# A quarter of each low part in the stage over v moves from VectorE to GpSimd

## The chip, the cores and the metric

The kernel runs on one core of a Trainium2 chip. A core has five engines that work side by side and wait for each other through semaphores: TensorE (PE; its weight loads are listed apart as PEld), VectorE (DVE), ScalarE (ACT), GpSimd (POOL) and SyncE (SP), which here only issues transfers. The metric is the device time of one execution in microseconds (us); lower is better. It is measured as the median of several executions. A profile is one execution, and its own time stands beside its span (first to last instruction).

## The reference

Two transformer blocks over a sequence of 512 tokens with 1024 features. The first block has a stick-breaking attention, a short convolution and a mixture of experts. The second block has attention, a Hyena filter and, at its end, the PEER layer, in which the change lies:

```python
def chunk(xc):                                   # 128 tokens
    q = (xc @ wq).reshape(PEER_CHUNK, PEER_HEADS, 2, half)
    s1 = jnp.einsum('chd,hnd->chn', q[:, :, 0], keys1)
    s2 = jnp.einsum('chd,hnd->chn', q[:, :, 1], keys2)
    ...                                          # 16 best pairs for each token and head: eidx, g
    a = jnp.einsum('chkd,cd->chk', u_tab[eidx], xc)
    wgt = (jax.nn.gelu(a) * g)
    return jnp.einsum('chk,chkd->cd', wgt, v_tab[eidx])
```

u_tab and v_tab have 16384 rows of 1024 numbers each.

## The kernel before, in words

For 384 of the 512 tokens the kernel does not gather rows. It multiplies by the whole of u and later by the whole of v, with a weight matrix that is zero where an expert was not chosen. For the other 128 tokens it gathers the rows of u and of v that each token needs, with indirect transfers that GpSimd issues (one transfer brings one row of 1024 for each of the 128 tokens, 0.5 MB; there are 128 for u and 128 for v).

**Parts.** A product in float32 is made of three products of a faster type, fp32r. Each operand is split in a high part (the value rounded to fp32r) and a low part (the value minus its high part). A *unit* is a tile of 128x2048 of wq, u or v. SP loads it in `RAW[n % 2]`; ScalarE makes the high part (`high`, line 1858) and VectorE the low part (`low`, one subtraction of 128x2048 through the helper `tt`, line 592), both in `PART[n % 2]`; TensorE then works on it. There are 8 units of wq, 64 of u and 64 of v. Everything is double buffered: `high(n)` and `low(n)` wait until TensorE has finished unit n-2, SP reloads `RAW` for unit n when the low part of unit n-2 is done.

**The stage over v** (from about 2146 us) has 32 steps of two units. For each unit TensorE makes 36 matmuls of 128x512 (lines 2648 to 2650). Here the first unit of a step is called the even unit and the second the odd one. The order of the work on every engine is one list written by hand, `V_STEPS`, that each engine's program walks through and of which it takes what is its own:

```python
for n in range(32):
    V_STEPS.append(("part", v_unit[n] + 1))          # odd unit of step n
    ...
    V_STEPS += [late.pop(0) for _ in range(2) if late] or [sums.pop(0) for _ in range(2) if sums]
    if n + 1 < 32:
        V_STEPS.append(("up", n + 1))
        V_STEPS.append(("part", v_unit[n] + 2))      # even unit of step n + 1
    V_STEPS += [late.pop(0) for _ in range(2) if late] or [sums.pop(0) for _ in range(4 if n % 3 == 0 else 3) if sums]
    V_STEPS.append(("down", n))
```

- "part": ScalarE `high`, VectorE `low`, SP the load of a later unit.
- "up": VectorE multiplies the tile `GIN` by the weights `WRB` (four instructions gin<-gin,wr of 128x384), ScalarE makes its high part `GE` (line 1944), VectorE its low part (four instructions ge<-gin,ge). SP loads `WRB` and `GIN` of a later step (`chunk`).
- "ud": a dot product of a gathered row of u (line 1375), in steps 0 to 5, four in each.
- "sv": a weighted sum of a gathered row of v (`row_sum`, line 600, tmp<-ug or vg,sparse,tmp, 128x1024). There are 128, in the steps after, five or six in each: two after the low part of the odd unit, and three (four in every third step) after the low part of the even unit. GpSimd, at the same place of its own list, issues the gather of the row eight sums later (`row_of_v`, line 2663), which waits until VectorE has made that sum.
- "down": the matmuls of the step.

In every instruction of VectorE named here both tensor inputs lie in SBUF.

**The other place that the diff touches** is far ahead, in the stage over the experts: ScalarE issues a load of ctx (1 MB, line 1639, semaphore `cx`) and four small loads of filter weights (lines 1640 to 1643, semaphore `lay`), and later squares ctx (`squares(10, ...)`, line 1488).

Of the kernel before, what the change touches and what calls it, by code (L numbers as in the profile page):

```python
# [74 lines left out]
def program(nc, A, out):  # L75
# [10 lines left out]
    ctx = ExitStack()  # L86
    with ctx:
# [5 lines left out]
        def sem(name):  # L93
# [2 lines left out]
        s = {n: sem("s_" + n) for n in (  # L96
            "const par z_v zd x0 x1 x2 x3 nsq nmm nv nw h_v pj_mm pj_a hn_v cv sc_a ada_v ada_mm ada_a att_mm att_a att_v "
            "mg_mm mg_v op_mm op_v wr rt_mm rt_v rt_a ht_mm ht_a hd mi_mm mi_a mi_v mu_mm mu_a mu_v mt_mm mm_v md_mm md_a md_v "
            "gx0 gx1 gx2 ys0 ys1 ys2 cx lay rope ly_mm ly_v ly_a xg xw xp xa xv xy gy0 gy1 gy2 gy3 cb_mm cb_v "
            "kv_mm kk_a hm_a kp_mm ro_mm ro_v w4_key fl_mm fl_v fl_a hp_mm hp_a hp_v tt_mm tt_a sp_mm sp_a sp_v iv_mm iv_v "  # L100
            "s2_mm e2_a a2_v tr_mm tr_a tr_v pv_mm pv_a gt_mm gt_a m2_mm m2_v o2_mm o2_v "
            "rw0 rw1 un_hi un_lo h2_v hr_a fx_mm fx_a gt0 gt1 gt2 gt3 sc_mm sc2_a tk_v tk_a tx_mm wg_v wg_mm wg_a ws0 ws1 "
            "wq0 wq1 gin0 gin1 gm_v ge_a vd_mm hs_a hs_mm ud_v ug0 ug1 ug2 ug3 sw_v vg0 vg1 vg2 vg3 ys_v y2_v fo_v out "
            "w0 w1 w2 w3 w4 w5 ph_a ph_v").split()}

# [416 lines left out]
        UNIT += [("v", c, h) for c in range(32) for h in range(2)]  # L522

        UNIT_DONE, n_fx, n_vd = [], 0, 0
        for kind, c, half in UNIT:
            if kind == "v":
                n_vd += 3
                UNIT_DONE.append(("vd_mm", n_vd))
            else:
                n_fx += 2  # L530
                UNIT_DONE.append(("fx_mm", n_fx))
# [56 lines left out]
        def vector_program(eng):  # L588
            dve = Port(eng)

            def tt(out_, in0, in1, op):
                return v.tensor_tensor(out=out_, in0=in0, in1=in1, op=op)  # L592
# [633 lines left out]
            def low(n):  # L1226
                if n < len(UNIT):
                    if n >= 2:
                        dve.wait_ge(s[UNIT_DONE[n - 2][0]], UNIT_DONE[n - 2][1])
                    dve.wait_ge(s["un_hi"], n + 1)  # L1230
                    hi, lo = PART[n % 2]
                    tt(lo, RAW[n % 2], hi.bitcast(f32), SUB).then_inc(s["un_lo"], 1)

            norm(18, 1.0 / D, S)
            for k in range(8):
# [221 lines left out]
            for half in range(2):  # L1457
                for q in (1, 3):
                    dve.wait_ge(s["vd_mm"], 6 * 31 + 3 * half + q)
                    dve.wait_ge(s["un_lo"], len(UNIT))  # L1460
                    if half and q == 3:
                        for d in (1, 2, 3):
                            sum_square(d, PA4, PV4)
                    v.tensor_copy(YT[q][:, 512 * half:512 * half + 512], bank[2 * (q - 1) + half]).then_inc(s["sw_v"], 1)
                for j in range(4):
                    d = 4 * half + j
                    dve.wait_ge(s["hs_mm"], 2 + d + 1)
                    stt(X[:, d, :], bank[(0, 2, 4, 6)[j] + half], MOD[:, 40 + d, 0:1], X[:, d, :], MUL, ADD).then_inc(s["y2_v"], 1)
                    if half and j:
                        sum_square(d - 1, PA4, PV4)  # L1470
                if half:
                    sum_square(7, PA4, PV4)
# [6 lines left out]
        def scalar_program(eng):  # L1479
# [156 lines left out]
            def layers(kind, li):  # L1636
                if kind == "dma" and li == 0:
                    act.wait_ge(s["op_mm"], 8)
                    a.dma_start(CX, A["ctx"].rearrange("p (k n) -> p k n", k=8)).then_inc(s["cx"], 16)
                    a.dma_start(ZF[0:33, :], A["zf"]).then_inc(s["lay"], 16)  # L1640
                    a.dma_start(FW1[0:33, :], A["hf_w1"]).then_inc(s["lay"], 16)
                    a.dma_start(FW2[0:64, :], A["hf_w2"]).then_inc(s["lay"], 16)
                    a.dma_start(FW3[0:64, :], A["hf_w3"]).then_inc(s["lay"], 16)
                if kind == "ctx":
                    squares(10, [CX[:, k, :] for k in range(8)], 256, lambda i: (s["cx"], 16))
                    root(10, 256)
                    act.wait_ge(s["ada_v"], 4)
                    for k in range(8):
                        act.wait_ge(s["h_v"], 17 + k)
                        a.activation(HC[:, k, :], HC[:, k, :], ACT.Identity, bias=MOD[:, k, 1:2]).then_inc(s["hm_a"], 1)  # L1650
                if kind == "sin":
                    act.wait_ge(s["ly_v"], 7 * li + 7)
                    a.activation(HM[0:64, :], ft[0][0:64, :], ACT.Sin).then_inc(s["ly_a"], 1)
                if kind == "dma" and li == 1:
                    act.wait_ge(s["ly_mm"], 3)
                    a.dma_start(COS, A["rope"][0]).then_inc(s["rope"], 16)
                    a.dma_start(SIN, A["rope"][1]).then_inc(s["rope"], 16)
                    a.dma_start(SKB, A["skip"]).then_inc(s["rope"], 16)
# [309 lines left out]
            for half in range(2):  # L1968
                act.wait_ge(s["vd_mm"], 6 * 31 + 3 * half + 2)
                act.wait_ge(s["un_lo"], len(UNIT))  # L1970
                if half:
                    square_chunks(19, "y2_v", PA4, PV4, 0, 4)
                a.activation(YT[2][:, 512 * half:512 * half + 512], bank[2 + half], ACT.Copy).then_inc(s["hs_a"], 1)
# [5 lines left out]
        def tensor_program(eng):  # L1979
# [223 lines left out]
            def layers(kind, li):  # L2203
                if kind == "ctx":
                    norm(10, ones, 256)
                if kind == "mm":
                    pe.wait_ge(s["lay"], 64)
                    pe.wait_ge(s["nv"], 41)
                    pe.wait_ge(s["ly_a"], li)
                    w, kk, src = ((FW1, 33, ZF), (FW2, 64, HM), (FW3, 64, HM))[li]  # L2210
                    t.matmul(bank[7][0:64, :], w[0:kk, :], src[0:kk, :], start=True, stop=True).then_inc(s["ly_mm"], 1)
# [419 lines left out]
            for kind, n in V_STEPS:  # L2631
# [3 lines left out]
                for half in range(2):  # L2635
                    unit = v_unit[n] + half
                    wh, wl = (k4(x) for x in PART[unit % 2])
                    pe.wait_ge(s["un_lo"], unit + 1)
                    pe.wait_ge(s["gm_v"], 8 * n + 8)
                    pe.wait_ge(s["fx_a"], len(fx_of))  # L2640
                    pe.wait_ge(s["sc2_a"], 16)
# [17 lines left out]
        def pool_program(eng):  # L2659
# [44 lines left out]
            def row_of_v(k):  # L2704
                if k < 128:
# [6 lines left out]
                        gp.wait_ge(s["wg_mm"], 96)  # L2712
                    rows(VG[(k + 4) % 8], A["v"], EID[:, k:k + 1], s[f"vg{k % 4}"])

            for kind, *i in ORDER3 + V_STEPS:
                if kind == "ud":
                    for k in range(4) if i[0] == 0 else (i[0] + 3,):
                        row_of_u(k)
                elif kind in ("vr", "sw"):
                    for k in range(4) if kind == "vr" else range(4, 8):  # L2720
                        row_of_v(k)
                elif kind == "sv":
                    row_of_v(i[0] + 8)


        def sync_program(eng):
# [66 lines left out]
            def unit(n):  # L2793
# [6 lines left out]
                    src = A["vd"][2 * c + half]  # L2800
                if n >= 2:
                    sp.wait_ge(s["un_lo"], n - 1)
                nc.sync.dma_start(RAW[n % 2], src).then_inc(s[f"rw{n % 2}"], 16)

            sp.wait_ge(s["o2_mm"], 8)
# [172 lines left out]
```

## Time and profile before

| what | value |
|---|---|
| median of 3 runs | 2714.17 us (2713.97 to 2717.03) |
| the profiled execution: time, span | 2714.08 us, 2712.3 us |
| mean granted clock of TensorE | 0.963 |
| busy over the span | PE 2480.9 us (91%), DVE 1712.5 us (63%), ACT 1044.2 us (38%), POOL 403.0 us (15%) |
| VectorE's low parts, all 136 units | 311.2 us, 2289 ns each |
| ScalarE's high parts, all 136 units | 260.5 us, 1915 ns each |

In the rows below a line of a timeline is: start (us from the span's start), duration (us), engine, line of the kernel, operation, output<-inputs, count; and in brackets the idle time of the engine just before and what ended it. Instructions of one engine that follow each other overlap a little in the records, so the step from start to start is the time that one costs in a chain. "part" is `PART`, "raw" is `RAW`, "P" is a PSUM bank, "tmp" is the sum over v, "ug" and "vg" are the eight buffers of gathered rows, "sparse" holds the weights of the sums.

### The profile page before, as it was taken

What the parts mean: (1) busy time and instruction counts of PE and PEld (TensorE: products, weight loads), DVE (VectorE), ACT (ScalarE), POOL (GpSimd) and SP (SyncE); (2) the same over time, 40 slices, a digit from 0 to 9 for tenths busy, and PEclk for the clock granted to TensorE, in tenths of its full rate; (3) what the DMA queues carried; (4) which work ended last, traced back from release to release, by engine and by line L of the source; (5) the groups of instructions that cost most, each with busy time, mean ns of one, the idle gap of its engine ahead of it and who ended that gap; (6) DMA issues with size and microseconds to landing.
All of it is one profiled execution on the core that took longest, in us unless ns stands there. A gap on an engine that the chain in (4) does not pass through costs nothing.

```text
span 2712.3 us, 31160 instructions
## 1 busy us (share of the span) xinstructions
PE 2480.9 (91%) x12293; PEld 1883.7 (69%) x12293; DVE 1712.5 (63%) x2974; ACT 1044.2 (38%) x1307; POOL 403.0 (15%) x299
## 2 busy tenths in 40 slices
PE   6998999587877989999989999989999999999996
PEld 4665676433333434577768999989999988777775
DVE  4524235412116556665642998889999478888886
ACT  4844532220104321377332433436555333333333
POOL 0100000000001000000000011232343134444430
PEclk9999999698986999999999999999999999999998
DMA  4443442499992100211122367769989799999992
GB/s 196 172 162 124 162 179 95 155 383 424 426 383 99 62 31 1 93 63 39 56 93 93 131 216 239 251 233 326 340 347 344 285 383 363 380 381 380 383 369 93
DMA packets 159215, 605.96 MB, mean 223 GB/s; under 512 B 13687, under 2 KB 79351, under 8 KB 126360
## 3 DMA queue, kind: packets, MB, share of 16 engines
q1 hardware_dynamic: 91104, 384.32, 37.8%
q0 software_dynamic: 42480, 154.68, 15.3%
q10 hardware_dynamic: 25480, 64.90, 6.1%
q8 instruction: 99, 1.62, 0.2%
q14 instruction: 52, 0.43, 0.0%
HBM read 533.08 MB, written 70.78 MB: 223 GB/s over the span
## 4 chain that ended last, share of the span: by engine, by line
PE 51%; DVE 21%; DMA 13%; issue 10%; ACT 4%; POOL 1%; ACTq 0%; SPq 0%; DVEq 0%; POOLq 0%
DVE window L592 6%; PE P L2544 4%; PE P L2545 4%; PE P L2546 4%; PE P L2200 4%; DVE part L592 3%; DMA ug<-in_v,sparse 3%; PE P L2375 3%; DVE ug L1375 3%; DMA H<-in_w_up 3%; PE P L2003 2%; DMA vg<-in_v,sparse 2%; PE P L2004 2%; PE P L2005 2%; DVE tmp L600 2%
## 5 line engine op out<-in xcount | busy, mean ns | idle before, releaser
L592 DVE TENSOR_TENSOR part<-raw,part 128x2048 fp32r<-128x2048 f32 x136 | 311.2, 2289 | 166.3 <-ACT part L1858 166.2
L2544 PE MATMUL P<-hr,part 128*128 128x384 f32 (+1 forms) x1136 | 397.8, 350 | 17.8 <-DVE part L592 17.1
L2546 PE MATMUL P<-hr,part 128*128 128x384 f32 (+1 forms) x1136 | 392.3, 345 | 0.0
L2545 PE MATMUL P<-hr,part 128*128 128x384 f32 (+1 forms) x1136 | 392.2, 345 | 0.0
L2663 POOL DMA_INDIRECT ug<-in_ur,sparse x128 | 177.5, 1387 | 1216.1 <-DVE window L1267 754.3
L2648 PE MATMUL P<-part,ge 128*128 128x512 f32 x768 | 301.8, 393 | 10.5 <-DVE part L592 9.8
L1858 ACT ACTIVATE part<-raw 128x2048 fp32r<-128x2048 f32 x136 | 260.5, 1915 | 101.7 <-PE P L2650 82.3
L2649 PE MATMUL P<-part,ge 128*128 128x512 f32 x768 | 299.1, 389 | 0.0
L2650 PE MATMUL P<-part,ge 128*128 128x512 f32 x768 | 298.9, 389 | 0.0
L2544 PEld LDWEIGHTS P<-hr,part 128*128 128x128 f32 x1136 | 215.3, 189 | 28.8 <-DVE part L592 22.9
L2545 PEld LDWEIGHTS P<-hr,part 128*128 128x128 f32 x1136 | 215.2, 189 | 4.8
L2546 PEld LDWEIGHTS P<-hr,part 128*128 128x128 f32 x1136 | 214.9, 189 | 4.9
L592 DVE TENSOR_TENSOR arena<-arena,P 128x512 f32<-128x512 f32 (+3 forms) x100 | 56.8, 577 | 207.6 <-ACT arena L1634 135.4
L2648 PEld LDWEIGHTS P<-part,ge 128*128 128x128 f32 x768 | 144.1, 188 | 49.0 <-DVE part L592 18.7
L1930 ACT ACTIVATE gt<-P 128x384 f32<-128x384 f32 x128 | 62.9, 492 | 296.8 <-PE P L2546 296.6
L1944 ACT ACTIVATE ge<-gin 128x384 fp32r<-128x384 f32 x128 | 65.5, 526 | 262.0 <-DVE gin L592 261.5
L2650 PEld LDWEIGHTS P<-part,ge 128*128 128x128 f32 x768 | 144.2, 188 | 30.2
L2649 PEld LDWEIGHTS P<-part,ge 128*128 128x128 f32 x768 | 144.2, 188 | 29.2
L1375 DVE SCALAR_TENSOR_TENSOR ug<-ug,ht 128x1024 f32<-128x1024 f32 x128 | 154.9, 1218 | 6.9 <-DMA ug<-in_ur,sparse 6.8
L2200 PE MATMUL P<-W,arena 128*64 128x512 f32 x384 | 124.8, 635 | 16.6 <-DMA H<-in_w_up 10.5
L592 DVE TENSOR_TENSOR window<-window 128x1024 bf16<-128x1024 bf16 (+6 forms) x198 | 118.4, 648 | 1.5
L2663 POOL DMA_INDIRECT vg<-in_v,sparse x64 | 101.6, 1588 | 116.0 <-DVE tmp L600 102.4
(359 smaller groups left out, 4483.7 us busy)
## 6 DMA issues: line engine op xcount, KB each, us to landing
raw<-in_u SPq DMA_DIRECT2D x64, 1024.0 KB, 5.3
raw<-in_vd SPq DMA_DIRECT2D x64, 1024.0 KB, 8.0
W<-in_w_up SPq DMA_DIRECT2D x24, 2048.0 KB, 18.3
W<-in_w_in SPq DMA_DIRECT2D x18, 2048.0 KB, 8.5
W<-in_ada_w SPq DMA_DIRECT2D x12, 2048.0 KB, 7.8
a_scratch<-gt ACTq DMA_DIRECT2D x128, 192.0 KB, 3.9
w_scratch<-window ACTq DMA_DIRECT2D x12, 2048.0 KB, 13.1
wr<-w_scratch SPq DMA_DIRECT2D x32, 768.0 KB, 13.4
```

The costliest lines, as they stand in the source:

```text
L592: return v.tensor_tensor(out=out_, in0=in0, in1=in1, op=op)
L1375: v.scalar_tensor_tensor(out=UG[k % 4], in0=UG[k % 4], scalar=1.0, in1=HT0, op0=MUL, op1=MUL, accum_out=DOT[:, k:k + 1]).then_inc(s["ud_v" ...
L1858: a.activation(PART[n % 2][0], RAW[n % 2], ACT.Copy).then_inc(s["un_hi"], 1)
L2200: ins = t.matmul(bank[2 + i % 2][xs, :], XT[i % 2][:, k, xs], w[:, k, :], start=k == 0, stop=k == 7)
L2375: ins = t.matmul(bank[n % 2], w[:, k, (n % 4) * 128:(n % 4) * 128 + 128], H[:, k, :], start=k == 0, stop=k == 7)
L2544: t.matmul(b, wh[:, k, js], HR[0][:, k, lo:S], start=k == 0, stop=False)
L2545: t.matmul(b, wh[:, k, js], HR[1][:, k, lo:S], start=False, stop=False)
L2546: ins = t.matmul(b, wl[:, k, js], HR[0][:, k, lo:S], start=False, stop=k == 7)
L2648: t.matmul(b, gh[:, k, qs], wh[:, k, :], start=n == 0 and k == 0, stop=False)
L2649: t.matmul(b, gh[:, k, qs], wl[:, k, :], start=False, stop=False)
L2650: ins = t.matmul(b, gl[:, k, qs], wh[:, k, :], start=False, stop=n == 31 and k == 3)
L2663: return g.indirect_dma_start(out=dst, out_offset=None, in_=src, in_offset=bass.IndirectOffsetOnAxis(ap=idx, axis=0)).then_inc(sem_, 16)
```

## The change

In the stage over v GpSimd makes columns 1536 to 2047 of the low part, and VectorE columns 0 to 1535. This holds for 63 of the 64 units; the first is left whole (`po_lo` gives 0 for it). GpSimd's instruction is queued at the place of "part" in its list and waits, as VectorE's does, for unit n-2 of TensorE and for the high part. It counts a semaphore of its own, `po_lo`, and all that waited for VectorE's half wait for it too: TensorE's matmuls of the unit, SP's reload of `RAW`, and at the end VectorE and ScalarE before they write over `RAW`. To have a semaphore for it, the load of ctx gives up its own (`cx`) and counts in `lay` with the four small loads, so that ScalarE's squares now wait for all five.

```diff
@@ -522,6 +522,7 @@
         UNIT_DONE, n_fx, n_vd = [], 0, 0
+        po_lo = lambda n: max(0, n - v_unit[0])
@@ -1229,7 +1230,8 @@
                     dve.wait_ge(s["un_hi"], n + 1)
                     hi, lo = PART[n % 2]
-                    tt(lo, RAW[n % 2], hi.bitcast(f32), SUB).then_inc(s["un_lo"], 1)
+                    m = 1536 if po_lo(n) else 2048
+                    tt(lo[:, 0:m], RAW[n % 2][:, 0:m], hi[:, 0:m].bitcast(f32), SUB).then_inc(s["un_lo"], 1)
@@ -1458,6 +1460,7 @@
                     dve.wait_ge(s["un_lo"], len(UNIT))
+                    dve.wait_ge(s["po_lo"], po_lo(len(UNIT) - 1))
@@ -1636,13 +1639,13 @@
-                    a.dma_start(CX, A["ctx"].rearrange("p (k n) -> p k n", k=8)).then_inc(s["cx"], 16)
+                    a.dma_start(CX, A["ctx"].rearrange("p (k n) -> p k n", k=8)).then_inc(s["lay"], 16)
...
-                    squares(10, [CX[:, k, :] for k in range(8)], 256, lambda i: (s["cx"], 16))
+                    squares(10, [CX[:, k, :] for k in range(8)], 256, lambda i: (s["lay"], 80))
@@ -1968,6 +1971,7 @@
                 act.wait_ge(s["un_lo"], len(UNIT))
+                act.wait_ge(s["po_lo"], po_lo(len(UNIT) - 1))
@@ -2204,7 +2208,7 @@
-                    pe.wait_ge(s["lay"], 64)
+                    pe.wait_ge(s["lay"], 80)
@@ -2636,6 +2640,8 @@
                     pe.wait_ge(s["un_lo"], unit + 1)
+                    if po_lo(unit):
+                        pe.wait_ge(s["po_lo"], po_lo(unit))
@@ -2712,7 +2718,16 @@
+            def low(n):
+                if n < len(UNIT):
+                    gp.wait_ge(s[UNIT_DONE[n - 2][0]], UNIT_DONE[n - 2][1])
+                    gp.wait_ge(s["un_hi"], n + 1)
+                    hi, lo = PART[n % 2]
+                    g.tensor_tensor(out=lo[:, 1536:2048], in0=RAW[n % 2][:, 1536:2048], in1=hi[:, 1536:2048].bitcast(f32), op=SUB).then_inc(s["po_lo"], 1)
+
             for kind, *i in ORDER3 + V_STEPS:
+                if kind == "part":
+                    low(*i)
@@ -2800,6 +2815,8 @@
                 if n >= 2:
                     sp.wait_ge(s["un_lo"], n - 1)
+                    if po_lo(n - 2):
+                        sp.wait_ge(s["po_lo"], po_lo(n - 2))
```

## Rows read from the trace of the kernel before

**Rows 1.** The windows of the stage: dots, sums, the last steps.

```profile
core 0: us, PE busy (x) PEld busy (x) DVE busy (x) ACT busy (x) POOL busy (x), PEclk, DMA share, GB/s
2126.00:2236.00 110.00, 108.72 (x503) 92.54 (x502) 79.13 (x107) 38.84 (x42) 34.76 (x24) 1.00 0.92 337
2241.40:2641.00 399.60, 390.35 (x1700) 317.02 (x1699) 353.84 (x360) 134.88 (x140) 187.56 (x124) 1.00 1.01 378
2641.00:2674.50 33.50, 33.50 (x148) 27.46 (x147) 24.40 (x27) 11.96 (x13) 0.00 (x0) 1.00 0.43 150
```

**Rows 2.** Who waited for whom in the sums' stretch: total us, times, longest us.

```profile
DVE part L592 <- ACT part L1858: 33.3, 25, 1.7
...
PEld P L2648 <- DVE part L592: 17.4, 22, 1.7
...
PE P L2648 <- DVE part L592: 9.2, 7, 1.3
```

**Rows 3.** VectorE's timeline: first, one whole, a longer and last of 23 steps with sums.

```profile
2257.84 2.29 DVE L592 TENSOR_TENSOR part<-raw,part 128x2048 fp32r<-128x2048 f32 x1 [1.32 <-ACT part L1858]
...
2343.36 2.29 DVE L592 TENSOR_TENSOR part<-raw,part 128x2048 fp32r<-128x2048 f32 x1 [1.32 <-ACT part L1858]
2345.57 4.06 DVE L600 SCALAR_TENSOR_TENSOR tmp<-ug,sparse,tmp 128x1024 f32<-128x1024 f32 x3
2349.55 2.29 DVE L592 TENSOR_TENSOR part<-raw,part 128x2048 fp32r<-128x2048 f32 x1
2351.75 2.67 DVE L600 SCALAR_TENSOR_TENSOR tmp<-vg,sparse,tmp 128x1024 f32<-128x1024 f32 x2
2354.34 1.02 DVE L592 TENSOR_TENSOR gin<-gin,wr 128x384 f32<-128x384 f32 x2
...
2359.91 2.29 DVE L592 TENSOR_TENSOR part<-raw,part 128x2048 fp32r<-128x2048 f32 x1 [1.31 <-ACT part L1858]
...
2377.85 2.29 DVE L592 TENSOR_TENSOR part<-raw,part 128x2048 fp32r<-128x2048 f32 x1 [1.31 <-ACT part L1858]
...
2649.61 2.29 DVE L592 TENSOR_TENSOR part<-raw,part 128x2048 fp32r<-128x2048 f32 x1 [1.32 <-ACT part L1858]
```

**Rows 4.** ScalarE's timeline: two odd units of the dots' steps, then an odd and an even.

```profile
2213.00 1.92 ACT L1858 ACTIVATE part<-raw 128x2048 fp32r<-128x2048 f32 x1 [4.57 <-PE P L2650]
...
2229.32 1.92 ACT L1858 ACTIVATE part<-raw 128x2048 fp32r<-128x2048 f32 x1 [4.32 <-PE P L2650]
...
2345.81 1.92 ACT L1858 ACTIVATE part<-raw 128x2048 fp32r<-128x2048 f32 x1 [2.55 <-PE P L2650]
...
2357.91 1.90 ACT L1858 ACTIVATE part<-raw 128x2048 fp32r<-128x2048 f32 x1
```

**Rows 5.** TensorE's weight loads that open an even unit, in two steps.

```profile
2345.71 0.19 PEld L2648 LDWEIGHTS P<-part,ge 128*128 128x128 f32 x1 [0.36 <-DVE part L592]
...
2380.19 0.19 PEld L2648 LDWEIGHTS P<-part,ge 128*128 128x128 f32 x1 [1.74 <-DVE part L592]
```

**Rows 6.** GpSimd's timeline over the step of rows 3.

```profile
2347.12 1.93 POOL L2663 DMA_INDIRECT ug<-in_v,sparse  x1 [6.82 <-DVE tmp L600]
2349.36 1.08 POOL L2663 DMA_INDIRECT ug<-in_v,sparse  x1 [0.30 <-issue]
2350.74 1.90 POOL L2663 DMA_INDIRECT ug<-in_v,sparse  x1 [0.30 <-issue]
```

**Rows 7.** Groups by form: the same kind of subtraction on VectorE over fewer columns.

```profile
L592 DVE TENSOR_TENSOR arena<-arena 128x512 f32<-128x512 f32 x54 | 36.1, 689 | 1.4 <-ACT arena L1740 0.3
...
L592 DVE TENSOR_TENSOR Wr<-W,tr 128x1024 fp32r<-128x1024 f32 x18 | 21.9, 1220 | 4.2 <-ACT tr L1808 4.2
```

**Rows 8.** VectorE's timeline in a step of the dots: the odd unit.

```profile
2231.34 2.29 DVE L592 TENSOR_TENSOR part<-raw,part 128x2048 fp32r<-128x2048 f32 x1 [1.66 <-ACT part L1858]
```

**Rows 9.** ScalarE's timeline in the experts' stage: load of ctx, first squares.

```profile
560.61 0.36 ACTq L1639 DMA_DIRECT2D arena<-in_ctx  x1
...
573.59 0.71 ACT L1488 ACTIVATE tmp<-arena 128x256 f32<-128x256 f32 x2
```

More of the change, by code:

```diff
@@ L98, in program @@
             "mg_mm mg_v op_mm op_v wr rt_mm rt_v rt_a ht_mm ht_a hd mi_mm mi_a mi_v mu_mm mu_a mu_v mt_mm mm_v md_mm md_a md_v "
-            "gx0 gx1 gx2 ys0 ys1 ys2 cx lay rope ly_mm ly_v ly_a xg xw xp xa xv xy gy0 gy1 gy2 gy3 cb_mm cb_v "
+            "gx0 gx1 gx2 ys0 ys1 ys2 lay rope ly_mm ly_v ly_a xg xw xp xa xv xy gy0 gy1 gy2 gy3 cb_mm cb_v "
             "kv_mm kk_a hm_a kp_mm ro_mm ro_v w4_key fl_mm fl_v fl_a hp_mm hp_a hp_v tt_mm tt_a sp_mm sp_a sp_v iv_mm iv_v "
             "s2_mm e2_a a2_v tr_mm tr_a tr_v pv_mm pv_a gt_mm gt_a m2_mm m2_v o2_mm o2_v "
-            "rw0 rw1 un_hi un_lo h2_v hr_a fx_mm fx_a gt0 gt1 gt2 gt3 sc_mm sc2_a tk_v tk_a tx_mm wg_v wg_mm wg_a ws0 ws1 "
+            "rw0 rw1 un_hi un_lo po_lo h2_v hr_a fx_mm fx_a gt0 gt1 gt2 gt3 sc_mm sc2_a tk_v tk_a tx_mm wg_v wg_mm wg_a ws0 ws1 "
             "wq0 wq1 gin0 gin1 gm_v ge_a vd_mm hs_a hs_mm ud_v ug0 ug1 ug2 ug3 sw_v vg0 vg1 vg2 vg3 ys_v y2_v fo_v out "
```

## The prediction

> **What bounds the kernel now.** The page says that TensorE is busy nearly all the time in the stage over v. I first cut the stage in windows [rows 1]. In the stretch with the dots TensorE is busy 108.7 of 110 us, in the last steps all 33.5 us. In the stretch with the sums it is busy 390.35 of 399.6 us, so about 9 us are free there, and VectorE works 353.8 us. The granted clock is 1.00 in all three, the upper level, so no time can come from the clock. The waits say who holds TensorE up [rows 2]: only VectorE's low part, 17.4 + 9.2 us. TensorE alone needs 16.32 us for a step: two odd units in the dots' stretch wait for its matmuls 2213.00 to 2229.32 [rows 4].
>
> The loop that sets the pace with the sums is read from the timelines. VectorE starts the even low part at 2343.36, then come three sums, the odd low part (2349.55), two sums, and the chain of gin and ge (from 2354.34); the next even low part starts at 2359.91, after 16.55 us [rows 3]. It has one pause in there, 1.31 us, and that ends with ScalarE's high part. That high part itself started at 2357.91, behind the last ge of ScalarE and not behind TensorE [rows 4]. So the loop runs VectorE, ScalarE, VectorE: TensorE isn't in it and is made to wait, 0.36 us in a short step and 1.74 us in a step with a fourth sum [rows 5], which takes 17.94 us (2359.91 to 2377.85). From 2257.84 to 2649.61 there are 23 such periods, 15 short and 8 long: 15 x 16.55 + 8 x 17.94 = 391.8 us, which is what the two starts are apart [rows 3]. A microsecond more or less per period on VectorE is 23 us.
>
> **The change, part by part.**
>
> *Removed from VectorE.* The subtraction takes 689 ns over 512 columns, 1220 over 1024 [rows 7], 2290 over 2048 [rows 3]: 1.04 ns a column. A quarter of 2048 is worth 0.53 us; 1536 columns take 1.76 us. Two units in a period: 1.07 us less.
>
> *Added on GpSimd, its own price.* The trace has no instruction of GpSimd over a tile. Lower bound: VectorE's price for the same 512 columns, 0.69 us [rows 7]. Upper bound: GpSimd's longest usual instruction, a gather, 1.93 us [rows 6]. I take 1.25 us, near the middle, since no row is nearer to one end. The Trainium skill, GPSIMD Engine Reference, section "Elementwise — side-by-side cycle accounting", gives 4497 ns against VectorE's 2293 for a tensor_tensor of 2048 fp32 columns. VectorE's figure agrees with the 2289 of this trace; no row here shows GpSimd's. By a quarter of it, an estimate of 1.12 us, the sum below would be 28 us instead of 34.
>
> *Added: what GpSimd's instruction does to VectorE.* Both halves wait for the same high part and read the same two tiles, and every instruction of VectorE in the stage reads two SBUF tiles. No row shows the two engines computing together. The bounds are 0 (side by side) and the whole of GpSimd's instruction (VectorE stands still for it). I take the whole: VectorE leaves hardly a gap behind its low part in which the other could be served without holding anything up [rows 3], and the two ask in the same instant. The Trainium skill, SBUF — State Buffer, section "Who interferes with whom", says that a VectorE instruction with two SBUF inputs contends with a GpSimd one that reads SBUF, and that the one that issues second is blocked for the whole of the first. No row here shows that. By it the sum is the one I give; without it, it would be that of the first rival.
>
> *The period then.* Even unit: VectorE's 1.76 us first, GpSimd's 1.25 behind it, then the sums: 0.72 us later than now, and the even part is ready 0.72 us later. Odd unit: VectorE goes on, 1.76, and its sums follow. GpSimd is not there yet. Its list puts the gathers of the three sums first; in the trace the last of them ends at 2352.64, while VectorE's odd part was ready at 2351.84 [rows 3, 6]. So GpSimd's quarter lands between or behind the next sums, and holds VectorE 1.25 us there: again 0.72 net. Period: 16.55 + 1.43 = 17.98 us, and 19.37 with the fourth sum. Over 23 periods: 23 x 1.43 = 32.9 us. At either end of the stretch a half period counts 0.72 more (the odd unit ahead of 2257.84, and the last even part, for which TensorE waits): 34.3 us.
>
> *Is the late odd part a loss of its own?* It is ready some 12.4 us after the even low part's start. TensorE begins the even unit at 3.0 and asks for the odd one after half of 16.32, at 11.2; it waits 1.2 us, and is done with it at 20.6. The next even part is ready at 17.98 + 3.0 = 21.0. It fits, with 0.4 us to spare: free as long as GpSimd's odd quarter isn't later than that. Behind it in GpSimd's list stand two gathers, which are needed eight sums later. Behind SP's longer wait stand the loads of RAW and of WRB and GIN; the odd ones start about 2 us later in a period that is 1.4 us longer. I cost both at nothing.
>
> *Dots and last steps.* In the dots' steps VectorE idles 1.66 us ahead of an odd low part, for a high part that waits for TensorE [rows 4, 8]. The two net 0.72 (1.43 us) lie in that pause. Nothing. The last steps have no sums behind the odd unit and TensorE is busy throughout [rows 1]. Nothing.
>
> *The semaphore of ctx.* The load of ctx starts at 560.61, the squares at 573.59 [rows 9]. They wait for four small loads as well, issued right behind it. At most 1 us on ScalarE, which isn't the bound there. Nothing.
>
> Sum, against the profiled execution's 2714.08 us (the runs' median is 2714.17, the same): 2714.1 + 34.3 = **2748.4 us**.
>
> **The rivals.**
>
> *Side by side (faster).* GpSimd's quarter costs VectorE nothing. Then VectorE's period is 15.48 us, or 16.87 with the fourth sum, on average 15.96; that is below TensorE's 16.32, so TensorE becomes the bound: 23 x 16.32 = 375.4 instead of 391.8, 16.4 us less, 2697.7 us. GpSimd's late odd quarter wouldn't spoil it, since VectorE gains a lead on TensorE of some microseconds. For it: the two are different engines, and GpSimd is idle nearly half of the stretch. Against it: the transfers. Their share is already 1.01 at 378 GB/s [rows 1]; the same bytes in 383 us are 394 GB/s. It decides if GpSimd holds VectorE for less than 0.53 us an instruction; at just that the time is unchanged.
>
> *A short hold (no change).* GpSimd is near its lower bound of 0.69 us, or holds VectorE only for a part of it: 46 x (0.6 - 0.53) = 3 us; or side by side, but the transfers give nothing more. 2711 to 2719 us.
>
> *GpSimd is starved (much slower).* VectorE's instructions follow each other without a pause until the one of 1.31 us; if GpSimd gets its turn only there, the even part is ready after 14 to 16 us instead of 2.3. TensorE's even unit then ends at 15 + 8.2 = 23, ScalarE's next high part at 25: a period of 25 us, 23 x 8.5 = 195 us more, 2910 us. In a milder form only the odd quarter comes later than its 0.4 us to spare: 1 us late in each period is about 14 us on top, 2762 us. Against it: between two sums VectorE waits for its own semaphore, which gives GpSimd a door.
>
> *The change does nothing* can't be: 63 instructions are moved to another engine in the loop that sets the pace.
>
> **How the numbers follow.** The hold: 0.70. Its own range goes by GpSimd's price from 0.95 to 1.75 us: 46 x 0.42 + 1.4 = 21 to 46 x 1.22 + 1.4 = 57, so 2735 to 2771 us. Side by side 0.13, no change 0.10, starved 0.07, half of it mild. A measurement of this kernel can tell about 0.2%, 5.4 us, from no change. Faster 0.13, same 0.10, slower 0.77. The range of 8 in 10 takes in the hold, no change and the mild form, and ends at 2712 and 2776 us.
>
> **What would show it.** Right: VectorE's part<-raw,part over 1536 columns at 1.76 us; low part to first sum of an even unit 2.9 to 3.1 us instead of 2.21; even low parts 18.0 and 19.4 us apart; TensorE waits for GpSimd's part at both units; the dots' stretch unchanged. Wrong: even low parts 16.3 us apart (side by side); a GpSimd part that ends only in VectorE's pause (starved); an even period that is longer than VectorE's own sum explains (the late odd part). If VectorE's own instructions read longer in the records instead of starting later, the hold is there all the same, inside them.

## The result and the profile after

The changed kernel takes 2754.97 us (median of 4 runs, 2753.96 to 2756.16), beside 2714.61 us for the kernel before on the same chip. The ratio is 1.0142, with a 95% interval of 1.0125 to 1.0158: 40 us slower, where 34 were forecast. The profiled execution took 2753.96 us with a span of 2752.1, against the 2712.3 of before.

The groups show the split low part: the new one of GpSimd, and VectorE's part over 1536 columns (from the groups by form of 2120 to 2720 us, as is the third line, half of the sums).

```profile
L2726 POOL TENSOR_TENSOR part<-raw,part 128x512 fp32r<-128x512 f32 x63 | 140.6, 2232 | 184.1 <-ACT part L1861 176.5
L593 DVE TENSOR_TENSOR part<-raw,part 128x1536 fp32r<-128x1536 f32 x63 | 112.8, 1790 | 56.1 <-ACT part L1861 53.4 <-PE P L2656 2.6
L601 DVE SCALAR_TENSOR_TENSOR tmp<-vg,sparse,tmp 128x1024 f32<-128x1024 f32 x63 | 103.3, 1640 | 3.3
```

VectorE's own part is as short as forecast (1.79 us instead of 2.29). But its sums, which nobody touched, read 1640 ns each (those from vg) and 1598 (from ug) instead of 1282 and 1283, and GpSimd's 512 columns read 2232 ns, though the shortest of the 63 took 1295. The timelines show why. VectorE's first, with one short step and the start of the next (compare [rows 3]):

```profile
2350.59 1.76 DVE L593 TENSOR_TENSOR part<-raw,part 128x1536 fp32r<-128x1536 f32 x1 [1.32 <-ACT part L1861]
2352.26 5.07 DVE L601 SCALAR_TENSOR_TENSOR tmp<-vg,sparse,tmp 128x1024 f32<-128x1024 f32 x3
2357.25 1.75 DVE L593 TENSOR_TENSOR part<-raw,part 128x1536 fp32r<-128x1536 f32 x1
2358.92 1.28 DVE L601 SCALAR_TENSOR_TENSOR tmp<-vg,sparse,tmp 128x1024 f32<-128x1024 f32 x1
2360.30 2.13 DVE L601 SCALAR_TENSOR_TENSOR tmp<-ug,sparse,tmp 128x1024 f32<-128x1024 f32 x1
2362.36 1.01 DVE L593 TENSOR_TENSOR gin<-gin,wr 128x384 f32<-128x384 f32 x2
...
2367.93 1.76 DVE L593 TENSOR_TENSOR part<-raw,part 128x1536 fp32r<-128x1536 f32 x1 [1.32 <-ACT part L1861]
```

GpSimd's over the same step (compare [rows 6]):

```profile
2350.63 2.85 POOL L2726 TENSOR_TENSOR part<-raw,part 128x512 fp32r<-128x512 f32 x1 [3.10 <-ACT part L1861]
2354.83 1.94 POOL L2669 DMA_INDIRECT vg<-in_v,sparse  x1 [1.35 <-DVE tmp L601]
2357.07 1.08 POOL L2669 DMA_INDIRECT vg<-in_v,sparse  x1 [0.30 <-issue]
2358.46 1.35 POOL L2669 DMA_INDIRECT vg<-in_v,sparse  x1 [0.30 <-issue]
2359.83 1.51 POOL L2726 TENSOR_TENSOR part<-raw,part 128x512 fp32r<-128x512 f32 x1
```

In the even unit both records start at 2350.6. VectorE's instruction takes its undisturbed 1.76 us; GpSimd's record runs to 2353.48, 1.13 us past VectorE's end; and the three sums behind take 5.07 us where they took 4.06. So GpSimd waits for VectorE, and then VectorE stands still for 1.01 us inside its own record. In the odd unit GpSimd comes 2.6 us after VectorE, behind its gathers, and the sum that it meets reads 2.13 us for 1.28: 0.85 more. Together 1.86 us are held for 1.07 saved. The step takes 17.34 us (2350.59 to 2367.93) instead of 16.55.

TensorE's weight load that opens this even unit comes when GpSimd's piece is ready, and had waited 1.39 us where it waited 0.36 [rows 5]:

```profile
2353.55 0.19 PEld L2654 LDWEIGHTS P<-part,ge 128*128 128x128 f32 x1 [1.39 <-issue]
```

The windows answer to [rows 1]: dots, sums, last steps. TensorE is now idle 27.5 us of the sums' 415.7 instead of 9.3 of 399.6, at the same granted clock of 1.00.

```profile
2135.00:2252.00 117.00, 110.34 (x500) 92.78 (x498) 81.27 (x103) 38.83 (x42) 63.95 (x36) 0.99 0.87 311
2264.30:2680.00 415.70, 388.22 (x1673) 312.74 (x1673) 369.35 (x357) 133.15 (x139) 277.20 (x171) 1.00 0.98 362
2680.00:2714.00 34.00, 33.00 (x146) 26.98 (x146) 24.38 (x27) 11.58 (x13) 9.89 (x4) 1.00 0.41 142
```

Only a part of the 39.8 us of span is in the sums. Both traces are cut here at the same events:

| stretch | before | after | more |
|---|---|---|---|
| up to the first matmul of the stage over v | 2146.5 | 2155.2 | 8.7 |
| first odd low part to that of step 6, counted from 0 (dots) | 98.9 | 106.9 | 8.0 |
| from there to the last low part (sums, last steps) | 423.0 | 446.2 | 23.2 |

The 8.7 us ahead of the stage begin at the semaphore of ctx. The load is issued at 562.21, the squares start at 582.60, 20.4 us later instead of 13.0 [rows 9], and what ended ScalarE's wait was one of the small loads behind ctx. TensorE waited 8.21 us for the squares. ScalarE's timeline (ACTq is its DMA issue), then TensorE's:

```profile
562.21 0.36 ACTq L1642 DMA_DIRECT2D arena<-in_ctx  x1
...
582.60 0.72 ACT L1491 ACTIVATE tmp<-arena 128x256 f32<-128x256 f32 x2 [7.32 <-DMA arena<-in_hf_w]
583.07 6.32 PE L1992 MATMUL P<-tmp,cst 128*128 128x256 f32 x16 [8.21 <-ACT tmp L1491]
```

In the dots' stretch VectorE stands longest before one dot, for a gathered row:

```profile
2187.14 2.31 DVE L1377 SCALAR_TENSOR_TENSOR ug<-ug,ht 128x1024 f32<-128x1024 f32 x1
...
2197.24 1.23 DVE L1377 SCALAR_TENSOR_TENSOR ug<-ug,ht 128x1024 f32<-128x1024 f32 x1 [7.79 <-DMA ug<-in_ur,sparse]
```

The rows are gathered and used in the same order, and the dot at 2197.24 is the 17th from the last; so its gather is the 17th from the last gather of u, the one at 2184.11 in GpSimd's timeline. It stands behind the odd low part of the step before (2.63 us, of which a part is the wait for VectorE) and four gathers of rows of v:

```profile
2174.11 2.63 POOL L2726 TENSOR_TENSOR part<-raw,part 128x512 fp32r<-128x512 f32 x1
...
2184.11 0.94 POOL L2669 DMA_INDIRECT ug<-in_ur,sparse  x1 [0.30 <-issue]
2185.35 0.94 POOL L2669 DMA_INDIRECT ug<-in_ur,sparse  x1 [0.30 <-issue]
2186.30 2.06 POOL L2726 TENSOR_TENSOR part<-raw,part 128x512 fp32r<-128x512 f32 x1
```

It was issued 3.0 us ahead of the dot before it (2187.14), where the same gather of before was 5.4 us ahead (2172.10 and 2177.54); and the row was used 12.2 us after the end of its gather, against 8.3 before. TensorE then waited 3.30 us for VectorE's next low part. The same place of before had a stall of 2.77 us. In sem_only and sums_only below, where GpSimd does no low part among the dots, it had 4.09 and 5.58 us: so the larger part of this one stall scatters from run to run. Four shorter waits (0.91, 2.45, 0.40 and 0.99 us) have no counterpart before. Each is for a row whose gather stands right behind a low part of GpSimd and ended only 5.4 to 5.9 us ahead of the dot; before, all but the gather of the stall ended 10 us ahead or more.

The first step with sums that counts in the prediction's 23 took 20.45 us (2275.02 to 2295.47) for 17.94, and the next 19.03 for 16.56. GpSimd's list shows why: the even low part stands behind a gather that waited 5.35 us until an earlier row had landed, and TensorE, whose weight load follows here, waited 4.96 us for GpSimd's piece. VectorE's piece had been ready since 2276.78.

```profile
2274.10 0.94 POOL L2669 DMA_INDIRECT vg<-in_v,sparse  x1 [0.74 <-issue]
2280.39 1.18 POOL L2669 DMA_INDIRECT vg<-in_v,sparse  x1 [5.35 <-DMA ug<-in_v,sparse]
2281.59 1.68 POOL L2726 TENSOR_TENSOR part<-raw,part 128x512 fp32r<-128x512 f32 x1
```

```profile
2283.34 0.19 PEld L2654 LDWEIGHTS P<-part,ge 128*128 128x128 f32 x1 [4.96 <-issue]
```

### The profile page after: what moved, and what is told of

It is laid out like the page before. It is cut to its first block, busy times and chain, and to the rows that moved or that the text cites. A ratio compares the mean times of both kernels' runs of the same rounds, so it can differ in the third digit from the quotient of the medians.

```text
span 2752.1 us, 31381 instructions
## 1 busy us (share of the span) xinstructions
PE 2493.7 (91%) x12293; PEld 1890.8 (69%) x12293; DVE 1736.8 (63%) x2974; ACT 1044.6 (38%) x1307; POOL 533.2 (19%) x362
## 4 chain that ended last, share of the span: by engine, by line
PE 53%; DVE 23%; issue 9%; DMA 8%; ACT 5%; POOL 2%; ACTq 0%; DVEq 0%; SPq 0%; POOLq 0%
DVE window L593 6%; PE P L2548 4%; PE P L2550 4%; PE P L2549 4%; DVE part L593 3%; PE P L2204 3%; DVE tmp L601 3%; PE P L2379 3%; DMA W<-in_w_up 3%; DVE ug L1377 3%; PE P L2007 2%; PE P L2008 2%; PE P L2009 2%; PE P L2654 2%; PE P L2655 2%
## 5 line engine op out<-in xcount | busy, mean ns | idle before, releaser
L593 DVE TENSOR_TENSOR part<-raw,part 128x2048 fp32r<-128x2048 f32 (+1 forms) x136 | 279.6, 2057 | 163.2 <-ACT part L1861 157.3
L2726 POOL TENSOR_TENSOR part<-raw,part 128x512 fp32r<-128x512 f32 x63 | 140.6, 2232 | 184.1 <-ACT part L1861 176.5
L1377 DVE SCALAR_TENSOR_TENSOR ug<-ug,ht 128x1024 f32<-128x1024 f32 x128 | 165.8, 1302 | 15.7 <-DMA ug<-in_ur,sparse 15.6
L2669 POOL DMA_INDIRECT arena<-h_rows,arena x16 | 15.0, 939 | 589.2 <-DMA h_rows<-arena 411.0
```

What stands on the lines that cost most here:

```text
L1377: v.scalar_tensor_tensor(out=UG[k % 4], in0=UG[k % 4], scalar=1.0, in1=HT0, op0=MUL, op1=MUL, accum_out=DOT[:, k:k + 1]).then_inc(s["ud_v" ...
L2669: return g.indirect_dma_start(out=dst, out_offset=None, in_=src, in_offset=bass.IndirectOffsetOnAxis(ap=idx, axis=0)).then_inc(sem_, 16)
L2726: g.tensor_tensor(out=lo[:, 1536:2048], in0=RAW[n % 2][:, 1536:2048], in1=hi[:, 1536:2048].bitcast(f32), op=SUB).then_inc(s["po_lo"], 1)
```

## The experiments

The theory after the result had three terms: the hold, that is the time for which VectorE stands still while GpSimd's instruction runs (A1), the semaphore of ctx (A2), GpSimd's list in the dots' stretch (A3). Eleven kernels took them apart. "Before" is always the kernel before on the same chip; ratios have their 95% interval. Stretches and timelines are from one profiled execution of each kernel.

**sem_only.** The changed kernel's three lines on ctx alone; GpSimd does no low part.

```
+ a.dma_start(CX, ...).then_inc(s["lay"], 16)          # was s["cx"]
+ squares(10, ..., lambda i: (s["lay"], 80))           # was (s["cx"], 16)
+ pe.wait_ge(s["lay"], 80)                             # was 64
```

> The kernel before with one edit: the load of ctx counts in the semaphore of the four small loads, and ScalarE's squares wait for all five. Theory A, the edit costs time of its own: in the changed kernel the squares began at 582.60, 20.4 us after the load of ctx, against 13.0 us before; the experts' stage waits behind them. 7 to 9 us more than the kernel before, 2722 us. Rival: the shift of 8 to 9 us that the changed kernel had ahead of the stage over v is a scatter from execution to execution; then this kernel takes 2714 to 2716 us.

2727.5 us against 2717.49, ratio 1.0027 (1.0016 to 1.0038). ScalarE's timeline shows the place:

```profile
564.14 0.36 ACTq L1639 DMA_DIRECT2D arena<-in_ctx  x1
...
584.96 0.72 ACT L1488 ACTIVATE tmp<-arena 128x256 f32<-128x256 f32 x2 [7.74 <-DMA arena<-in_hf_w]
```

By the interval, 4 to 10 us are lost by the semaphore alone (7 us by the ratio, 10 by the medians). The dots' stretch of this kernel, whose program there is that of before, took 102.8 us instead of 98.9: it scatters by about 4 us.

**own_sem.** The changed kernel with GpSimd's low parts counted on `cx`, from 16 on, and ctx back on `cx` alone.

```
+ po_lo = lambda n: 16 + n - v_unit[0] if n > v_unit[0] else 0
+ a.dma_start(CX, ...).then_inc(s["cx"], 16)
+ squares(10, ..., lambda i: (s["cx"], 16))
+ g.tensor_tensor(out=lo[:, 1536:2048], ..., op=SUB).then_inc(s["cx"], 1)
```

> The changed kernel, but the load of ctx keeps its own semaphore, on which GpSimd's low parts count on from 16; nothing else differs. Theory A: the changed kernel's time less the 8 us of the shared semaphore, 2746 to 2748 us; the stage over v begins when it does in the kernel before (first part of the stage ready near 2146 us) and takes 31 us more than there. Rival, scatter: 2755 us as the changed kernel.

2739.75 us against 2717.49, 1.0090 (1.0070 to 1.0111). The squares are back at 13.0 us after ctx (562.36, 575.34), the stage over v starts at 2144.4. So the squares' wait is the shared semaphore's. What it costs is less sharp: in the eleven kernels whose ctx has its own semaphore, TensorE's first weight load of the stage over v comes at 2144.3 to 2151.4 us (2146.5 in the kernel before), in the two where it is shared at 2155.1 and 2157.6. The dots took 108.7 us, the sums and last steps 442.2. The time is 6 us below the 2746 expected, and by the ratios 14 us below the changed kernel, give or take 7. All other kernels below except two_pieces stand on this one.

**no_pool.** GpSimd's low part and all waits for it removed, VectorE's 1536 columns kept; the last quarter of 63 low parts is left out.

```
  for kind, *i in ORDER3 + V_STEPS:
-     if kind == "part":
-         low(*i)
```

> As own_sem, but GpSimd makes nothing and nobody waits for it: the last 512 columns of 63 low parts are left out. This is what the change would give if GpSimd's instruction cost VectorE nothing and were never late. Theory A (VectorE was the bound with the sums, TensorE is next at 16.32 us a step): 23 periods of 16.32 instead of 391.8 us together, 16 us less than before, 2698 us. Rival: the transfers are at their limit at 378 GB/s, then 2710 to 2714 us.

2701.12 us against 2717.49, 0.9943 (0.9926 to 0.9959). The window of the sums:

```profile
2241.40:2641.00 399.60, 399.60 (x1764) 330.92 (x1764) 341.89 (x375) 141.72 (x146) 174.40 (x124) 1.00 1.03 388
```

TensorE is busy in all of it, and the transfers give 388 GB/s where they gave 378 [rows 1]. The side-by-side rival's arithmetic was right: 16 us are what VectorE's short part is worth if GpSimd's costs nothing. The transfers did not stand in the way.

**write_only.** GpSimd only writes zeros in its quarter; the last quarter of 63 low parts is left out.

```
- g.tensor_tensor(out=lo[:, 1536:2048], in0=RAW[..], in1=hi[..], op=SUB)
+ g.memset(lo[:, 1536:2048].bitcast(f32), 0.0)
```

> As own_sem, but GpSimd fills its 512 columns with zeros (an instruction that reads nothing from SBUF) instead of making the low part; the last quarter of 63 low parts is left out. Theory A, the hold is over the path by which both engines read SBUF: no instruction of VectorE is longer than before, sums stay at 1.28 us, and only GpSimd's place in its list can make it late: 2698 to 2706 us. Rival B, any instruction of GpSimd on SBUF holds VectorE: VectorE's sums are stretched by GpSimd's duration as in own_sem, and the time is above 2714 us.

2707.37 us against 2717.49, 0.9967 (0.9955 to 0.9980). VectorE's timeline shows three sums in 4.05 us right behind a low part beside which GpSimd wrote:

```profile
2342.34 1.76 DVE L593 TENSOR_TENSOR part<-raw,part 128x1536 fp32r<-128x1536 f32 x1 [1.53 <-ACT part L1861]
2344.01 4.05 DVE L601 SCALAR_TENSOR_TENSOR tmp<-ug,sparse,tmp 128x1024 f32<-128x1024 f32 x3
```

A written quarter holds nobody: the sums read 1281 to 1283 ns each. It isn't the same instruction, though: it takes 0.53 us and not 1.30. The kernel is 6 us slower than no_pool, just above the 2698 to 2706 expected; its sums don't explain that, and ScalarE waited 8.4 us for loads of `RAW` in the sums' stretch. In the dots' stretch VectorE waited 12.2 us for gathered rows, as much as in the changed kernel (12.5), and yet the stretch took 99.7 us: rows that come late cost little by themselves.

**sums_only.** GpSimd helps only from step 7 on (counted from 0), so the dots' stretch is before's.

```
+ po_lo = lambda n: 17 + n - v_unit[7] if n >= v_unit[7] else 0
```

> As own_sem, but GpSimd makes its quarter only from step 7 on, in the steps with the sums; the steps with the dots are as before. Theory A: the 10 us that the changed kernel lost between 2155 and 2263 us come from GpSimd's instructions among the dots. They go: 2746 less 10, some 2737 us, and the rest over before, about 20 us, is 22 periods of 0.8 to 1.0 us. Rival: the loss there is carried by something else (transfers, start of the stage) and stays: 2746 us.

2739.11 us against 2716.77, 1.0074 (1.0057 to 1.0092). The dots took 102.8 us, as in sem_only; sums and last steps 442.4, as in own_sem. So GpSimd's low parts cost the sums about 19 us. For the dots these two traces give 108.7 - 102.8, about 6 us; the four traces without a low part of GpSimd there (before, sem_only, no_pool, sums_only) lie at 98.0 to 102.8, three with all of them (changed, half, own_sem) at 106.9 to 108.7. The times alone don't separate sums_only from own_sem: their intervals overlap.

**gathers_first.** In GpSimd's list alone, the gathers of a dot's rows are moved ahead of the low part.

```
+ while x[0] == "ud" and at and G_STEPS[at - 1][0] in ("part", "vr"):
+     at -= 1
+ G_STEPS.insert(at, x)
```

> As own_sem, but in the steps with the dots GpSimd's list has the gathers of u ahead of its low parts; every instruction is kept. Theory A, the loss among the dots is lateness in GpSimd's queue (a low part waits for its high part with a gather behind it, and a dot then waits 7.8 us for its row): most of the 8 us stall goes, 2738 to 2741 us. Rival B, it is the hold on VectorE (the dots are stretched to 2.3 us): nothing changes, 2746 us, since as many instructions are held as in own_sem.

2754.93 us against 2716.77, 1.0132 (1.0113 to 1.0151): by the ratios 11 us worse than own_sem, where a gain was expected. The dots took 114.6 us for 108.7, the rest 447.0 for 442.2. The two intervals (1.0113 and up, 1.0111 and down) only just part. Of the waits in that stretch, own_sem has this line, and gathers_first has none of its kind:

```profile
DVE ug L1377 <- DMA ug<-in_ur,sparse: 13.6, 5, 8.3
```

Gathers_first has these in its place (us in total, times, longest):

```profile
PEld P L2654 <- issue: 15.6, 8, 6.8
PE P L2654 <- issue: 12.6, 6, 6.4
ACT part L1861 <- DMA raw<-in_vd: 6.2, 3, 4.1
```

No dot waits for its row any more; now TensorE waits for the low part that stands behind the gathers, and the load of RAW behind it is late. Neither of the two orders is free: both kinds want GpSimd at the same time. No third order was tried.

**half.** GpSimd takes 1024 of the 2048 columns.

```
- m = 1536 if po_lo(n) else 2048
+ m = 1024 if po_lo(n) else 2048
```

> As own_sem, but GpSimd makes 1024 of the 2048 columns. Theory A, VectorE stands still for as long as GpSimd reads, about 1.0 us at 512 columns and 2.0 to 2.1 at 1024: a period gains 2 x (2.05 - 1.07) = 2.0 us against 0.8, 28 us more than own_sem, 2774 us or above if the odd part comes too late for TensorE. GpSimd's instruction alone is 2.2 to 2.4 us. Rival, the hold is a fixed handing over of about 1 us whatever the size: a period shrinks by 1.07 x 2 - 2 = 0.1 us and the time is 2714 to 2730 us.

2774.73 us (one run) against 2716.77. VectorE's timeline, then GpSimd's:

```profile
2366.69 1.22 DVE L593 TENSOR_TENSOR part<-raw,part 128x1024 fp32r<-128x1024 f32 x1 [1.32 <-ACT part L1861]
2367.83 6.16 DVE L601 SCALAR_TENSOR_TENSOR tmp<-ug,sparse,tmp 128x1024 f32<-128x1024 f32 x3
```

```profile
2366.73 3.40 POOL L2726 TENSOR_TENSOR part<-raw,part 128x1024 fp32r<-128x1024 f32 x1 [3.10 <-ACT part L1861]
```

Three sums take 6.16 us for 4.06: the hold is 2.10 us for an instruction that takes 2.41 alone, against 1.01 for one of 1.30. The hold grows by 1.09 us for 512 more columns, and VectorE's saving only by 0.53. It is a single run, with the 2774 us that Theory A gave.

**in_pause.** In even units ScalarE makes the last 512 columns of the high part first, in an instruction of its own, and GpSimd starts then, while VectorE is still waiting for the rest. Odd units are VectorE's alone.

```
+ a.activation(hi[:, 1536:2048], RAW[n % 2][:, 1536:2048], ACT.Copy).then_inc(s["un_hi"], 1)
+ a.activation(hi[:, 0:1536], RAW[n % 2][:, 0:1536], ACT.Copy).then_inc(s["un_hi"], 1)
```

> GpSimd makes its quarter of the even units only, and ScalarE makes that quarter of the high part first, in an instruction of its own, so that GpSimd reads while VectorE waits for the rest (the pause of 1.3 us ahead of each even low part). The odd units are whole on VectorE. Theory A: GpSimd's 1.1 us fit in the pause, VectorE's sums are not stretched, the even low part is 0.53 us shorter and ScalarE's second instruction costs 0.2: 23 x 0.33 = 8 us less than before, 2706 us. Rival: GpSimd starts too late and laps over VectorE's 1536 columns, which are then held for the rest of it: 2714 us or above.

2710.4 us against 2716.77, 0.9970 (0.9959 to 0.9981). GpSimd's and VectorE's timelines:

```profile
2360.83 1.30 POOL L2732 TENSOR_TENSOR part<-raw,part 128x512 fp32r<-128x512 f32 x1 [1.82 <-ACT part L1864]
```

```profile
2362.17 1.76 DVE L594 TENSOR_TENSOR part<-raw,part 128x1536 fp32r<-128x1536 f32 x1 [1.41 <-ACT part L1865]
2363.84 2.67 DVE L602 SCALAR_TENSOR_TENSOR tmp<-vg,sparse,tmp 128x1024 f32<-128x1024 f32 x2
```

GpSimd is done at 2362.13, VectorE starts at 2362.17 and its sums are not stretched (1282 and 1284 ns each). The same instruction on the same engine holds nobody when it lies in VectorE's pause.

**even_only.** The control for in_pause: own_sem, with GpSimd's quarter in even units only, beside VectorE as in the change.

```
+ po_lo = lambda n: 16 + (n - v_unit[0]) // 2 if n > v_unit[0] and (n - v_unit[0]) % 2 == 0 else 0
```

> As own_sem, but GpSimd makes its quarter of the even units only; unlike in_pause ScalarE's high part is one instruction. Theory A, what made in_pause faster is that GpSimd reads while VectorE pauses, not that it has half as many units: here each even unit is held 1.0 us against 0.53 us saved, 23 x 0.5 = 11 us more than before, 2727 us. Rival: the even unit's quarter is harmless and the loss was the odd unit's; then it is 2705 to 2710 us like in_pause.

2735.39 us against 2719.18, 1.0057 (1.0041 to 1.0074). VectorE's timeline:

```profile
2355.73 1.76 DVE L593 TENSOR_TENSOR part<-raw,part 128x1536 fp32r<-128x1536 f32 x1 [1.32 <-ACT part L1861]
2357.40 5.09 DVE L601 SCALAR_TENSOR_TENSOR tmp<-ug,sparse,tmp 128x1024 f32<-128x1024 f32 x3
2362.42 2.28 DVE L593 TENSOR_TENSOR part<-raw,part 128x2048 fp32r<-128x2048 f32 x1
```

The short step is 17.05 us, 0.50 more, and 23 of them are 11.5 us of the 15.5 (0.57% of 2719). Theory A had 11 us and 2727; the other 4 us lie within what the dots and the start of the stage scatter. Between this kernel and in_pause lie 0.9%, with the same pieces on the same engines. They differ in when GpSimd's piece runs, and in ScalarE's split; two_pieces tries the split alone.

**one_input.** GpSimd's instruction reads one tile instead of two (it multiplies `RAW` by zero; the last quarter of 63 low parts is left out).

```
- g.tensor_tensor(out=lo[:, 1536:2048], in0=RAW[..], in1=hi[..], op=SUB)
+ g.tensor_scalar(out=lo[:, 1536:2048], in0=RAW[..], scalar1=0.0, scalar2=None, op0=MUL)
```

> As own_sem, but GpSimd's instruction reads one tile (RAW times 0.0) instead of two; the last quarter of 63 low parts is left out. Theory A, the hold is GpSimd's reading from SBUF: VectorE's first sum is still stretched, by GpSimd's new duration (0.5 to 0.9 us). Rival B, only two tiles read on both sides hold each other: VectorE's sums stay at 1.28 us and the time is near write_only's, 2705 us.

2714.26 us (one run) against 2719.18. GpSimd's timeline, then VectorE's:

```profile
2351.83 3.06 POOL L2726 TENSOR_SCALAR part<-raw 128x512 fp32r<-128x512 f32 x1 [1.00 <-ACT part L1861]
```

```profile
2351.78 1.76 DVE L593 TENSOR_TENSOR part<-raw,part 128x1536 fp32r<-128x1536 f32 x1 [1.30 <-ACT part L1861]
2353.45 4.41 DVE L601 SCALAR_TENSOR_TENSOR tmp<-ug,sparse,tmp 128x1024 f32<-128x1024 f32 x3
```

The instruction is longer by itself (1.52 us at the shortest, for 1.30), it too waits for VectorE (it ends 1.35 us after it), and yet here the sums are stretched by 0.35 us only. Both theories missed: the hold goes neither by the length of GpSimd's instruction nor away with its second input.

**two_pieces.** The kernel before, GpSimd without low parts; in even units ScalarE and VectorE make the two parts in pieces of 1024 columns, so VectorE starts in its pause.

```
+ CUTS = (0, 1024, 2048)
+ for k, (i, j) in enumerate(zip(cut(n), cut(n)[1:])):
+     dve.wait_ge(s["un_hi"], hi_of(n) - len(cut(n)) + 2 + k)
+     ins = tt(lo[:, i:j], RAW[n % 2][:, i:j], hi[:, i:j].bitcast(f32), SUB)
```

> No GpSimd at all: the kernel before, but for the even units of the stage over v ScalarE makes the high part in two instructions of 1024 columns, and VectorE the low part in two that follow each other piece by piece, so that VectorE's pause of 1.3 us is used. Theory A: the even part is ready 0.8 us earlier for one more instruction on each engine; VectorE's period falls to about 15.75 and 17.14 us, TensorE's 16.32 becomes the bound, 23 x 16.32 = 375 us instead of 392: 2700 us, as no_pool. Rival: the second instruction of ScalarE and VectorE costs as much as the overlap gives, 2710 to 2717 us.

2705.64 us against 2719.18, 0.9951 (0.9937 to 0.9964), the best version that computes everything, between the 2700 us of its theory and the 2710 of its rival. VectorE's pause ahead of the even low part is 1.08 us and 0.46 in two successive steps, instead of 1.31 [rows 3]:

```profile
2356.10 2.36 DVE L595 TENSOR_TENSOR part<-raw,part 128x1024 fp32r<-128x1024 f32 x2 [1.08 <-ACT part L1864]
...
2373.25 2.36 DVE L595 TENSOR_TENSOR part<-raw,part 128x1024 fp32r<-128x1024 f32 x2 [0.46 <-ACT part L1864]
```

So a part of in_pause's gain may be the split itself; what the quarter on GpSimd adds to it is not separated. The intervals of the two ratios, 0.9951 and 0.9970, overlap; GpSimd's help brings nothing that can be seen here.

## Why the prediction came out nearly right

**The bound and the period: right.** Time moved as VectorE's loop moved; TensorE waits for the low part at the even units, now for GpSimd's piece of it (a part of these waits is put down as "issue", at the moment when GpSimd's piece ends). No_pool shows the other end: with VectorE relieved, TensorE is the bound, at 16.4 us a step on average.

**The hold: the mechanism right, the size off.** "I take the whole: VectorE leaves hardly a gap" said that VectorE stands still for all of GpSimd's instruction. Half, in_pause and even_only show that VectorE is held, for longer when GpSimd's piece is larger, and only where the two meet. That it goes by what GpSimd reads rests on write_only (0) and one_input (0.35 us), whose instructions differ from the change's in more than the reading. The rule of the Trainium skill that the prediction weighed, in SBUF — State Buffer, "Who interferes with whom", says the same, and the trace agrees in direction: GpSimd's instruction ends 1.13 us after VectorE's, and the next of VectorE is stretched by 0.85 to 1.01 us. In size it does not agree: the hold is less than the whole of the instruction. The mis-sized term is "GpSimd's 1.25": its instruction takes 1.30 us alone, as good as forecast, but VectorE is held for 0.93 on average. The steady step is 0.79 us longer instead of 1.43, and 23 x 0.79 is 18 us where 32.9 stood. The sums' stretch still gave 23 us, since some steps took longer: 20.45 us for 17.94 and 19.03 for 16.56 where GpSimd's even piece came late and right after, and two late ones 17.59 for 16.56. Own_sem and sums_only have 19 in the same stretch.

**Two terms taken as nothing: wrong.** The first is "At most 1 us on ScalarE, which isn't the bound there. Nothing." The small loads were issued right behind ctx but the last landed some 20 us after it, not 13; TensorE waited 8.21 us for the squares, and the stages ahead of v ended 8.7 us later. Sem_only puts 4 to 10 us on it; in own_sem the squares are back at 13.0 us. The second is the dots: "The two net 0.72 (1.43 us) lie in that pause. Nothing." The stretch took 8.0 us more in this trace, of which up to 4 can be scatter; about 6 by sums_only. What the prediction left out is that the dots' gathers and GpSimd's low parts share one list and wait for each other in it. Gathers_first shows that turning their order round doesn't help. The gathers' lateness alone isn't it either: write_only keeps the order, its dots wait as long for their rows, and its stretch takes 99.7 us. So GpSimd's long reading piece is needed for the loss; how much of it is the hold (a dot reads 2.31 us for 1.22) and how much the piece's time in the list was not separated.

So the total is near by luck: one term is 11 to 15 us too large, and two that were put at nothing come to some 15 together.

**The late odd part: right, for a third of the steps.** The prediction had it ready 12.4 us after the even low part's start, with TensorE waiting 1.2 us and nothing lost. In eight of the steps with sums, seven of them with a fourth sum, TensorE starts the odd unit 12.25 to 12.28 us after the even low part's start and has waited 1.24 to 1.28 us. Such a step is 18.72 us for 17.94: its 0.78 more is what every step has, so the wait is free there. The eighth, without a fourth sum, is one of the two of 17.59 us, 0.24 above the others. In the other steps with sums TensorE never waits ahead of the odd unit. TensorE's weight loads show one such step (its even low part starts at 2385.28), even unit and odd:

```profile
2388.25 0.19 PEld L2654 LDWEIGHTS P<-part,ge 128*128 128x128 f32 x1 [1.16 <-issue]
...
2397.53 0.19 PEld L2654 LDWEIGHTS P<-part,ge 128*128 128x128 f32 x1 [1.27 <-issue]
```

**Rivals.** "Side by side" fell by the stretched sums, and its 16 us turned up in no_pool. "A short hold" is half true: 0.93 is short of 1.25 but above the 0.53 at which the change would have been even. "Starved" fell in its main form: GpSimd got its turn as soon as VectorE's instruction ended. A piece of GpSimd that came late cost time in one step and the next all the same, but it was late behind a gather and not behind VectorE.

**Open.** Why VectorE is held about 0.3 us less than GpSimd's instruction takes (1.01 for 1.30, 2.10 for 2.41), why 0.85 in the odd unit, why a one-tile read holds it 0.35 us only, and why the row that the late gather waited for landed late. None of these was tried further.

## What to carry to other kernels

A second engine that takes a share of the bound engine's work must be priced by what the bound engine loses while the two meet, and not only by the share: here 0.93 us lost for 0.53 saved with each instruction. Look for a pause of the bound engine and give the helper its input early enough to run there; here the bound engine could use the pause itself, by beginning on half a tile (two_pieces). Then ask what stood in the helper's list behind the new work, and when two loads are put on one semaphore, what the slowest of them waits for.

## What the runs showed of the hardware

- A GpSimd tensor_tensor over 128x512 fp32 took 1.30 us alone, over 128x1024 2.41. One that read a single tile through tensor_scalar was slower, 1.52 us for 512 columns; a memset of 512 took 0.53.
- GpSimd's instruction waited for VectorE's running one (1.76 us in it) with its record already open, and VectorE's next one was then held inside its record: 1.01 us for 512 columns, 2.10 for 1024, 0.35 when GpSimd read one tile, none when it only wrote (by a memset). So a hold is seen as a longer mean of an instruction that wasn't changed, and not as idle time.
- Of four small loads issued within 2.1 us behind a load of 1 MB, the last had landed only 20 us after that load was issued (20.4 and 20.8 us in two traces, by the start of the squares that waited for them).
